# Forgetting attention in a two-block transformer kernel: two pairs of buffers for sums and outputs, and the next weights split inside the step sequence

## What is computed

```python
def forgetting_attention(q, k, v, f_logit):
    log_f = jax.nn.log_sigmoid(f_logit.astype(jnp.float32)).transpose(0, 2, 1)
    cf = jnp.cumsum(log_f, axis=-1)
    ...
        s = jnp.einsum('bhqd,bhkd->bhqk', qb, k, preferred_element_type=jnp.float32) * scale
        s = s + cq[..., :, None] - cf[..., None, :]
        s = jnp.where(kpos[None, :] <= qpos[:, None], s, NEG_INF)
        p = jax.nn.softmax(s, axis=-1)
        return jnp.einsum('bhqk,bhkd->bhqd', p.astype(v.dtype), v)
...
    return jnp.concatenate([pool_out, attn_out], axis=-1) @ w_out
```

## Time and profile before

| | us |
|---|---|
| median of 3 runs | 2789.45 (2789.31 to 2793.49) |
| the profiled execution, its own time | 2789.42 |
| its span, first to last instruction | 2787.6 |
| PE busy | 2695.0 (97%) |
| DVE busy | 1398.9 (50%) |
| ACT busy | 955.4 (34%) |
| POOL busy | 194.2 (7%) |
| attention's steps, first to last matmul | about 1829 to 1997 |

### The profile page before, as it was taken

How to read it: one execution, slowest core, us unless ns; L and a number is a source line. 1 busy time by engine, 2 the same in 40 slices (tenths; PEclk the granted TensorE clock), 3 DMA queues, 4 the chain that set the end, 5 groups by cost and what they waited for, 6 DMA issues and landing times.

```text
span 2787.6 us, 31396 instructions
## 1 busy us (share of the span) xinstructions
PE 2695.0 (97%) x12432; PEld 2166.7 (78%) x12432; DVE 1398.9 (50%) x2147; ACT 955.4 (34%) x1566; POOL 194.2 (7%) x161
## 2 busy tenths in 40 slices
PE   6999999999999999999999999998999999999997
PEld 5766688888788778888888887965688888788886
DVE  3222223323534876664555544155468666466655
ACT  4333322223213555552001142355336655500001
POOL 0000000000020100000000010133020000000002
PEclk9999999999999999999999999999999999999999
DMA  3111111101422334546443431111214454644432
GB/s 144 61 61 64 66 46 38 39 31 61 150 69 105 138 117 158 173 164 249 158 159 136 147 104 50 40 35 27 76 61 150 145 166 158 227 164 169 168 133 106
DMA packets 98162, 314.60 MB, mean 113 GB/s; under 512 B 11072, under 2 KB 11328, under 8 KB 91232
## 3 DMA queue, kind: packets, MB, share of 16 engines
q1 hardware_dynamic: 98016, 312.59, 32.5%
HBM read 217.06 MB, written 92.34 MB: 111 GB/s over the span
## 4 chain that ended last, share of the span: by engine, by line
PE 74%; issue 14%; DVE 5%; ACT 4%; POOL 2%; DMA 2%; SPq 0%; POOLq 0%; ACTq 0%; DVEq 0%
PE bank L559 22%; PE bank L561 21%; PE bank L560 21%; PE bank L1005 2%; PE bank L693 1%; ACT p L1146 1%; DVE wlo L1569 1%; PE bank L956 1%; POOL accX L2240 1%; POOL accX L2231 1%; PE bank L982 1%; PE bank L620 1%; PE bank L957 1%; PE bank L737 1%; PE bank L983 1%
## 5 line engine op out<-in xcount | busy, mean ns | idle before, releaser
L559 PE MATMUL bank<-whi,ub 128*128 128x512 f32 x1024 | 405.1, 396 | 2.6 <-DMA ub<-ud_d 1.8
L561 PE MATMUL bank<-whi,ub 128*128 128x512 f32 x1024 | 404.4, 395 | 0.0
L560 PE MATMUL bank<-wlo,ub 128*128 128x512 f32 x1024 | 404.3, 395 | 0.0
L1045 ACT ACTIVATE whi<-raw 128x1024 fp32r<-128x1024 f32 x166 | 170.9, 1052 | 636.3 <-PE bank L561 623.0
L1569 DVE TENSOR_TENSOR wlo<-raw,whi 128x1024 fp32r<-128x1024 f32 x166 | 200.2, 1226 | 356.0 <-ACT whi L1045 356.0
L1804 DVE TENSOR_TENSOR accX<-bank,accX 128x512 f32<-128x512 f32 x288 | 194.4, 690 | 146.1 <-PE bank L561 145.7
L559 PE MATMUL bank<-hhi,whi 128*128 128x512 f32 x608 | 253.4, 417 | 5.5 <-DVE wlo L1569 3.7
L561 PE MATMUL bank<-hhi,wlo 128*128 128x512 f32 x608 | 240.1, 395 | 0.0
L560 PE MATMUL bank<-hlo,whi 128*128 128x512 f32 x608 | 239.7, 394 | 0.0
L559 PEld LDWEIGHTS bank<-whi,ub 128*128 128x128 f32 x1024 | 193.1, 189 | 48.8 <-issue 2.7
L561 PEld LDWEIGHTS bank<-whi,ub 128*128 128x128 f32 x1024 | 193.1, 189 | 44.8
(11 more groups left out here) (370 smaller groups left out, 5545.0 us busy)
## 6 DMA issues: line engine op xcount, KB each, us to landing
raw<-wp_d SPq DMA_DIRECT2D x166, 512.0 KB, 3.6
ub<-ud_d SPq DMA_DIRECT2D x64, 1024.0 KB, 8.6
ud_d<-h SPq DMA_DIRECT2D x128, 256.0 KB, 2.9
ud_d<-l SPq DMA_DIRECT2D x128, 256.0 KB, 3.4
rawp<-wp_d SPq DMA_DIRECT2D x26, 1024.0 KB, 6.4
gs<-sg_d SPq DMA_DIRECT2D x16, 512.0 KB, 3.9
xd_d<-accX SPq DMA_DIRECT2D x16, 512.0 KB, 2.7
sg_d<-sig SPq DMA_DIRECT2D x13, 512.0 KB, 2.6
```

The costliest lines, as they stand in the source:

```text
L559: e.matmul(P, sh, mh, start=first, stop=False, skip_group_check=more)
L560: e.matmul(P, sh, ml, start=False, stop=False, skip_group_check=more)
L561: return e.matmul(P, sl, mh, start=False, stop=last, skip_group_check=more)
L1045: e.activation(whi[n % SLOTS][:, :], raw[n % RAWS][:, :], ACT.Copy).then_inc(*up("whi", n))
```

## The change

The change has four parts.

- `rl` and `ov` get a second buffer each. The second pair lies in the third raw buffer (`raw[(CAT + 5) % 3]`, which piece 125 would take), and item idx uses pair idx % 2. ACT's first copy waits for the `clo` of two items back; for item 1 it waits for `wlo` of piece 122, the last that used that raw buffer.
- ACT's and POOL's parts of `tail` let six steps go by instead of three. DVE's part stays.
- ACT and DVE are no longer released after `pooled(3)`. They stay held through attention, and `weights(n)` calls `feed.ahead(CAT + SPLIT_STEPS[n])`, a count that grows by one at n = 9, 10, 11, 18 and 20. SP's feed is bounded at 120 before v_2 (its own counter is at 121 then, so `fetch(123)` is out), at 122 after `duplicates(1)` (piece 124), and is freed behind `clo` of the last item, ahead of the row blocks that follow the first three; there it fetches 125 to 127.
- `maxima_due` issues one product fewer up to each of n = 0 to 3 and has caught up at n = 4 with two in one step, and the negated maxima of item 1 are transposed at n = 6 instead of 7.

```diff
+CAT = 120
...
+SPLIT_STEPS = [sum(n >= first for first in (9, 10, 11, 18, 20)) for n in range(len(STEPS))]
...
 def maxima_due(n):
     if n < 7:
-        return min(16, 10 + (5 * n + 8) // 4)
+        return min(16, 10 + (5 * n + 4) // 4)
...
 def negated_at(n):
-    if n == 7:
+    if n == 6:
         return 1
...
-    rl = at("rl", HO + 60, [128, 512])
-    ov = at("ov", HO + 62, [128, 512])
+    RO2 = RO + 4 * ((CAT + 5) % RAWS)
+    rl = [at(f"rl{i}", kb, [128, 512]) for i, kb in enumerate((HO + 60, RO2))]
+    ov = [at(f"ov{i}", kb + 2, [128, 512]) for i, kb in enumerate((HO + 60, RO2))]
...
     # ACT and DVE, pooled(g)
-            if g == 3:
-                feed.held = False
-                feed.ahead(feed.cur + SLOTS)
...
     # ACT, weights(n)
+            feed.ahead(CAT + SPLIT_STEPS[n])
...
     # ACT, values(n)
                 if j == 0:
-                    e.wait_ge(*(ok("clo", idx - 1) if idx else ok("full", "pw", 3, 1)))
-                e.activation(rl[own, :], O[o:o + 64, :], ACT.Copy)
-                e.activation(ov[own, :], O[own, :], ACT.Copy).then_inc(*free("ov", idx, j))
+                    e.wait_ge(*(ok("clo", idx - 2) if idx > 1 else ok("wlo", CAT + 2) if idx else ok("full", "pw", 3, 1)))
+                e.activation(rl[idx % 2][own, :], O[o:o + 64, :], ACT.Copy)
+                e.activation(ov[idx % 2][own, :], O[own, :], ACT.Copy).then_inc(*free("ov", idx, j))
...
     # ACT and POOL, tail(idx)
-            yield
-            yield
-            yield
+            yield from idle(6)
...
     # DVE
-        attention_order(maxima, nothing, lambda t: idle(8), nothing, nothing, tail, pooled)
+        attention_order(maxima, nothing, lambda t: idle(8), lambda n, *_: feed.ahead(CAT + SPLIT_STEPS[n]), nothing, tail, pooled)
+        feed.held = False
...
     # SP
         fetch_c(0)
+        feed.cap = CAT
         for vh in range(2):
             run(token_major(feed, nothing, "v_2", 256 * vh, None))
...
         fetch_c(1)
         duplicates(1)
+        feed.cap = CAT + 2
+        feed.ahead(feed.cap)
...
         row(4, lg)
         row(5, lb)
+        e.wait_ge(*ok("clo", 7))
+        feed.cap = NPIECES
+        feed.ahead(CAT + 5)
```

More of the change, by code:

```diff
@@ L1531, in tail @@
                 e.wait_ge(*ok("qm", t, 1, 1))
-            e.activation(chi[4 + t][:, 512 * Q:512 * Q + 512], ov[:, :], ACT.Copy).then_inc(*up("cho", idx))
+            e.activation(chi[4 + t][:, 512 * Q:512 * Q + 512], ov[idx % 2][:, :], ACT.Copy).then_inc(*up("cho", idx))
         attention_order(lambda idx: idle(8), negated, stack, weights, values, tail, pooled)
+        feed.held = False
         def l_scale(dst, topic, scaled, *first):
@@ L2115, in tail @@
         def tail(idx):
+            r, o = rl[idx % 2], ov[idx % 2]
             for q in range(2):
@@ L2119, in tail @@
                     e.wait_ge(*ok("free", "ov", idx, 1))
-                e.reciprocal(rl[:, c], rl[:, c]).then_inc(*up("rl", idx, q))
+                e.reciprocal(r[:, c], r[:, c]).then_inc(*up("rl", idx, q))
                 yield
             e.wait_ge(*ok("rl", idx, 1))
-            e.tensor_tensor(out=ov[:, :], in0=ov[:, :], in1=rl[:, :], op=ALU.mult).then_inc(*up("on", idx))
+            e.tensor_tensor(out=o[:, :], in0=o[:, :], in1=r[:, :], op=ALU.mult).then_inc(*up("on", idx))
             yield
-        attention_order(maxima, nothing, lambda t: idle(8), nothing, nothing, tail, pooled)
+        attention_order(maxima, nothing, lambda t: idle(8), lambda n, *_: feed.ahead(CAT + SPLIT_STEPS[n]), nothing, tail, pooled)
+        feed.held = False
         def seeded(t, c):
@@ L2299, in tail @@
             c = slice(512 * Q, 512 * Q + 512)
-            yield
-            yield
-            yield
+            yield from idle(6)
             e.wait_ge(*ok("cho", idx))
             e.wait_ge(*ok(*latest))
-            e.tensor_tensor(out=clo[4 + t][:, c], in0=ov[:, :], in1=chi[4 + t][:, c].bitcast(F32),
+            e.tensor_tensor(out=clo[4 + t][:, c], in0=ov[idx % 2][:, :], in1=chi[4 + t][:, c].bitcast(F32),
                             op=ALU.subtract).then_inc(*up("clo", idx))
```

## The result

The changed kernel takes 2773.03 us as a median (2772.02 to 2773.98, 5 runs), the kernel before beside it 2792.66 (2789.31 to 2793.49, 5 runs). The ratio is 0.9935, 95% interval 0.9922 to 0.9948: faster by 0.65%. The forecast was 2774.1. The profiled execution took 2772.79 with a span of 2771.0, against 2789.42 and 2787.6: 16.6 us apart, where 15.3 were forecast. The medians are 19.6 apart, since the profiled execution of before lies at the low end of its five times. Other executions of that kernel show a mean granted clock of 0.990 with 2796.05 and of 0.993 with 2787.28, those of the changed kernel 0.993 to 0.994.

What follows compares the result with a forecast made beforehand. TensorE, busy nearly throughout, bounds the kernel; in attention only four stretches have holes, behind ACT or DVE queues. 4.4 + 7.8 + 4.8 - 1.4 - 0.3 = 15.3 us off 2789.42 gives 2774.1 us, range 2770 to 2783.

Steps and rivals of the forecast that it cites:

- the four stretches: Start of attention and third, fifth and seventh items: the only places in attention where TensorE was said to stand still.
- Splits and transposes at the start: Start of attention: moving splits and transposing negated maxima earlier removes holes of 2.33 and 2.30 us, gaining 4.4 us.
- The wait of 0.2 for n4: Start of attention, step 6: TensorE ready near 1840.5, n4 near 1840.7, so 0.2 us of waiting.
- The step-8 product: Start of attention: QM done near 1842.7, TensorE at step 8 near 1843.0, so no wait.
- the 2.33: Start of attention: TensorE idle 2.33 us for a maximum reduction on DVE queued behind its splits; forecast to go.
- Two pairs and the later tail: Third, fifth and seventh items: holes of 2.72, 3.01 and 2.07 us go, gaining 7.8 us.
- 0.4 to spare: Third item: P(31) ends at 1887.9, TensorE is ready at 1888.3, so the hole goes with 0.4 us left.
- The clock: Third, fifth and seventh items: three slow stretches behind the holes go, 3 x 1.6 = 4.8 us gained.
- the first rival: Attention: remaining small holes and the new 1.4 us one still lower the clock, 4.8 not won; 2778.9 us, chance 0.22.
- The splits at their new place: Steps 18 and 19: DVE's split delays a reduction, making a new 1.4 us hole before the transposes; bounds 0 to 3.
- The later loads: w_out_2: pieces 125 to 127 fetched ahead of yr loads 3 to 7 delay yr(3), costing 0.3 us; bounds 0 and 3.
- the slower rival: w_out_2: late loads make TensorE stand still for each of five row blocks, 21.5 us lost; 2795.6 us, chance 0.06.

Runs made afterwards that it cites:

- two of its variants that have the second pair: Changed kernel with DVE's splits behind the reductions of steps 18 and 20: 2769.75 us; that plus negated maxima of items 3, 5, 7 one step later: 2773.99 us.
- both variants that clear the path of that reduction: Changed kernel with DVE's splits behind the reductions of steps 18 and 20: 2769.75 us; changed kernel with splits at n = 20 and 22 instead: 2772.11 us.

## Why the prediction was right

*The number.* Profile against profile it is 16.6 us where 15.3 were forecast. Median against median it is 19.6, 4.3 more than forecast. That 2774.1 lies only 1.1 from the measured 2773.03 is in part luck: the base of three runs, 2789.45, was 3.2 below the median of five runs, 2792.66, and this made up for most of what the forecast of the gain lacked.

*Reading the four stretches.* Right: 16.43 of the 16.6 us lie between step 0 and `w_out_2`, and all of it in the steps named.

*Splits and transposes at the start.* 4.4 forecast, 4.34 measured, but not in every step as worked out. The wait of 0.2 for n4 came: the transposes start 0.29 us behind the start of the product before them, where 0.07 was usual (1843.63 to 1843.70 before the change), and right after n4 is done at 1840.37. The step-8 product was to come without a wait, and it didn't. PE's timeline of both places:

```profile
1840.23 0.23 PE L990 MATMUL bank<-identb,maskb 128*128 128x128 bf16 x1
1840.52 0.60 PE L973 MATMUL bank<-ident,n 128*34 128x128 f32 x4
...
1841.71 1.08 PE L1010 MATMUL bank<-P,va 128*128 128x512 f32 x2
1842.85 0.47 PE L987 MATMUL bank<-QS,KH 128*128 128x512 f32 x1
```

The last row is step 8. It starts 1.14 us behind the values products, where 0.51 is enough at step 12 (1852.13 to 1852.64 before the change), and 0.15 behind the end of the last QM copy (1842.11 + 0.59), the same lag as before (0.14). So QM still holds PE there, by some 0.6 us where it was 2.8 before, and no idle time is shown for it. The forecast comes out because it counted the old hole by its idle time of 2.30 alone and left out about as much of the new wait. The split between the two edits was about right (2.3 each; 1.94 and 2.0 when one is undone), and the new count of maxima, which was to help with the first hole, is not needed for it (with the old count and the splits gone the hole stays away). One part of the mechanism was told too narrowly: I gave the 2.33 to DVE's reductions alone, and the run with splits at the start shows ACT's P just as late behind them.

*Two pairs and the later tail.* Right in place and nearly in size. P(31) was to end near 1887.9 with 0.4 to spare. It ended at 1884.83; step 24 came 3.10 us earlier than before, so that is 1887.9 on the old count, and PE shows no hole. But the 0.4 us to spare were not there: the product of step 33 starts at 1884.88, only 0.05 behind P(31), and 0.56 behind the values products before it, where 0.41 is enough at step 9 (1848.24 to 1848.65 before the change). ACT still holds that start, by 0.15 us. The forecast had taken the shown end of the values products for the time from which PE is ready, and PE is ready earlier. The run with one pair gives the holes back as 2.71, 3.01, 0.91 and 1.16, within 0.01 of before. The term that was mis-sized is what late P costs: I took the idle time shown, and it is less than the delay. In items three and five 0.23 us each come from the wait of step 32 for P(30), which stood behind chi before the change (1.38 us from step 31 to step 32 against 1.15). In the seventh the two products behind the holes were 1.48 and 1.32 us late for 0.92 and 1.15 of idle. Together the three items gave 13.6 us where 7.8 + 4.8 = 12.6 were forecast, and these hidden waits account for that 1.0.

*The clock.* The price was right: 1.6 forecast, 1.57 in both pairs of executions that differ in nothing else there. By the formula of the Trainium skill (TensorE: Matmul & The Clock Gate, section Terms) it would be an estimated 1.7, so the rows and the page are 0.1 apart, and the rows decide. The conditions were not as firm as I put them: in these traces holes of 2.33, 2.30 and 2.71 us left the clock up, and it fell behind 2.72, 3.01, 0.92 + 1.15, once behind 0.99 + 0.18 and once behind 1.53. So the first rival (the clock still falls) did not come true in the profile of the changed kernel, which has no slow stretch in attention, but slow stretches did follow the small holes in two of its variants that have the second pair. The Trainium skill (same page, section A second HAM failure mode: psum-queue depth-cycling, which is the one that the first rival meant) says that PE's short idles between groups of matmuls, if frequent, make the clock go up and down. These traces agree that short idles can do it, and show that the same ones mostly don't. Over whole executions the mean granted clock is 0.990 to 0.993 before and 0.993 to 0.994 after, and lower clocks go with longer times. That may be why the medians differ by 3 us more than the profiles, but it isn't shown: the other executions have no trace, and slow stretches come outside attention too, as the one at 2397 above.

*The splits at their new place.* 1.4 forecast, a hole of 1.36 measured and 1.53 in the steps (the rest is hidden as above), released by the reduction as worked out; both variants that clear the path of that reduction remove it.

*The later loads.* 0.3 forecast, no new hole measured (0.09 us more behind the first product of `w_out_2`). DVE waited for yr(3) 6.15 us where it had waited 1.98, and PE was full (timeline of DVE, table by stretches):

```profile
1997.41 3.74 DVE L2137 TENSOR_TENSOR accX<-bank,yr 128x512 f32<-128x512 f32 x6 [6.15 <-DMA yr<-yd_d]
```

```profile
1984.00:2000.00 16.00, 16.00 (x72) 13.27 (x71) 7.64 (x13) 0.63 (x1) 2.34 (x2) 1.00 0.81 303
```

On the old count that is 1997.41 + 16.69 = 2014.1, before the 2014.7 to 2015.5 that I allowed, and nothing of the slower rival came about. The loads' new place was not tried by itself.

## What to carry to other kernels

When an in-order engine waits, look at what is queued behind the wait: the 2.46 us for POOL's clo cost PE 2.72, the like of it came in three items of eight, and a second pair of small buffers took it away. A piece of background work that is placed by step number also has a place inside the step; behind the work that frees a bank it was free, ahead of it it cost 1.5 us. When you look for waits, compare the starts of the same product in two timelines, and don't rely on the idle time shown: in these traces PE waited 0.2 us for n4 and for P(30) and 0.6 us for QM with none shown, and 1.5 us where 0.9 was shown. And near any hole count a chance of 1.6 us for the clock.

## What the runs showed of the hardware

Holes of one size don't have one effect on TensorE's clock: 2.72 and 2.71 us in the same step of two executions gave 0.57 over 4 us in one and 1.00 in the other. What decides was not tested. In one execution a slow stretch of 0.57 followed holes of only 0.99 and 0.18 us, in another one hole of 1.53, each time in the fifth item, while equal holes in the third item of the same executions left the clock at 1.00.

A product that waits can start before the one ahead of it is shown to end, so a wait of 0.22 us (step 32) or about 0.6 us (step 8) leaves no idle time in the profile.
